# Decode gathers of eight keys a row instead of four, all rotary keys gathered too, and new waits ahead of the gathers

## The reference, cut to what matters

```python
ckv = jnp.concatenate([cache_ckv[layer, pt].reshape(past, KV_LORA), cn], axis=0)   # 4104 x 256
kr = jnp.concatenate([cache_kr[layer, pt].reshape(past, ROPE_DIM), kn], axis=0)    # 4104 x 32
scores = (jnp.einsum("bqhc,btc->bhqt", q_lat, ckv)
          + jnp.einsum("bqhr,btr->bhqt", q_rope, kr)) * MLA_SCALE
p = jax.nn.softmax(jnp.where(mask, scores, NEG_INF), axis=-1)
return jnp.einsum("bhqt,btc->bqhc", p, ckv)
```

## Time and profile before

| | us |
|---|---|
| median of 3 runs | 1426.12 |
| lowest, highest | 1425.38, 1431.34 |
| span of the profiled execution (first to last instruction) | 1420.3 |
| decode stage in it (first score matmul to the last of the values) | 423 to 634.7 |
| mean granted TensorE clock | 0.991 |

### The profile page before, as it was taken

How to read it: one execution, slowest core, us unless ns; L and a number is a source line. 1 busy time by engine, 2 the same in 40 slices (tenths; PEclk the granted TensorE clock), 3 DMA queues, 4 the chain that set the end, 5 groups by cost and what they waited for, 6 DMA issues and landing times.

```text
span 1420.3 us, 27840 instructions
## 1 busy us (share of the span) xinstructions
PE 1366.0 (96%) x11072; PEld 1198.0 (84%) x11072; DVE 851.7 (60%) x1672; ACT 519.4 (37%) x1105; POOL 247.6 (17%) x193
## 2 busy tenths in 40 slices
PE   7999989999988999998999999999999999999997
PEld 7999977766756565566999999999999999999885
DVE  3385358887676556546575857744444455568655
ACT  4221457666361322236333234434333342123100
POOL 3110037775542444401000000000000000000000
PEclk9999999999999999999999999999999999999999
DMA  6643020001372647668122131133333327452722
GB/s 237 201 151 104 1 89 1 1 1 40 127 262 65 199 150 232 217 253 316 46 55 82 45 91 46 45 99 101 110 98 101 119 91 267 159 200 75 267 89 75
DMA packets 108437, 174.36 MB, mean 123 GB/s; under 512 B 14002, under 2 KB 77298, under 8 KB 107028
## 3 DMA queue, kind: packets, MB, share of 16 engines
q1 hardware_dynamic: 98068, 136.92, 29.5%
q0 software_dynamic: 10240, 35.66, 7.7%
HBM read 138.49 MB, written 34.06 MB: 121 GB/s over the span
## 4 chain that ended last, share of the span: by engine, by line
PE 53%; DVE 0%; issue 0%; ACT 0%; DVEq 0%
PE ps L2501 36%; PE ps L2532 10%; PE ps L2566 6%; PE ps L2552 0%; DVE p_h L2874 0%; DVE p_h L2877 0%; DVE p_stats L2861 0%; DVE p_h L2857 0%; PE ps L2542 0%; DVE p_mv L2868 0%; ACT p_rt L2649 0%; DVE p_rs L2872 0%; DVE p_stats L2866 0%; DVE p_stats L2865 0%; DVE p_ve L2870 0%
## 5 line engine op out<-in xcount | busy, mean ns | idle before, releaser
L2501 PE MATMUL ps<-p_x,p_w 128*128 128x272 f32 x4032 | 506.7, 289 | 1.1 <-PEq L2032 0.7
L2501 PEld LDWEIGHTS ps<-p_x,p_w 128*128 128x128 f32 x4032 | 506.4, 188 | 1.4 <-issue 1.4
L2532 PE MATMUL ps<-p_uh,p_w 128*128 128x352 f32 (+1 forms) x576 | 141.9, 327 | 0.0
L1023 POOL TENSOR_SCALAR p_pr<-p_pr,p_rec 128x896 f32<-128x896 f32 (+3 forms) x64 | 112.6, 1769 | 133.0 <-DVE p_rec L987 132.7
L2751 DVE TENSOR_TENSOR p_w<-p_sum,p_w 128x512 fp32r<-128x512 f32 x94 | 65.0, 691 | 117.7 <-ACT p_w L1959 117.6
L1959 ACT ACTIVATE p_w<-p_wr 128x512 fp32r<-128x512 f32 x96 | 60.1, 627 | 131.4 <-PE ps L2532 76.0
L1572 PE MATMUL ps<-p_kT,p_q_rows 32*64 32x256 f32 x2048 | 90.7, 416 | 13.8 <-issue 9.2
L2532 PEld LDWEIGHTS ps<-p_uh,p_w 128*128 128x128 f32 x576 | 101.8, 188 | 0.0
L2532 PE MATMUL ps<-p_ul,p_w 128*128 128x352 f32 (+1 forms) x288 | 94.3, 328 | 0.0
L1572 PEld LDWEIGHTS ps<-p_kT,p_q_rows 32*64 32x64 f32 x2048 | 60.0, 144 | 40.7 <-issue 34.0
L2751 DVE TENSOR_TENSOR p_w<-p_wr,p_w 128x512 fp32r<-128x512 f32 x95 | 65.6, 690 | 38.0 <-ACT p_w L1959 37.4
(11 more groups left out here) (340 smaller groups left out, 2459.8 us busy)
## 6 DMA issues: line engine op xcount, KB each, us to landing
p_wr<-w_in SPq DMA_DIRECT2D x48, 512.0 KB, 3.6
g_kept<-p_slots SPq DMA_DIRECT2D x48, 272.0 KB, 2.5
p_ring<-g_kept SPq DMA_DIRECT2D x16, 544.0 KB, 5.1
p_x<-x_kept SPq DMA_DIRECT2D x6, 1088.0 KB, 8.1
t_kept<-p_t_raw SPq DMA_DIRECT2D x16, 272.0 KB, 2.4
p_x<-t_kept SPq DMA_DIRECT2D x4, 1088.0 KB, 9.3
p_gy<-g_kept SPq DMA_DIRECT2D x8, 544.0 KB, 6.2
p_xs<-x_prompt SPq DMA_DIRECT2D x8, 512.0 KB, 4.2
```

Of the source, the lines that this page charges most:

```text
L1023: nc.gpsimd.tensor_scalar(pr[:, n % PR, 0:w], pr[:, n % PR, 0:w], rec[:, n % PR:n % PR + 1], None, ALU.mult).then_inc(normed, 1)
L2501: last = pe.matmul(ps[:, lo + z, 0:PW], w[:, q % NW, part, t, :], v[:, t, z * PW:(z + 1) * PW], start=(i in STARTS and t == 0 and n == 0), ...
L2532: last = pe.matmul(ps[:, BANK_OF[g % 8], 0:tn], w[:, q % NW, part, t, :], v[:, t0:t0 + tn], start=(t == 0 and z == 0), stop=(t == KH - 1 a ...
```

## The change

A gather now brings rows of eight keys (`ROWK` = 8): 128 rows of 8 KB, 1 MB, for two groups; `h` counts such gathers, `NH` = 32. `NAT` is 10 slots of 1 MB, where it was 19 of 512 KB. The rotary keys come by one gather of 128 rows of 1 KB for each `h`, all on GpSimd; `load_rotary` is gone. In step n GpSimd waits for the whole scoring, gathers `h` = n/2 + 5 (latent and rotary), waits until half of the step's values are done, and gathers `h` = n/2 + 6. `mostly_scored` is gone. VectorE turns `keys(n + 6)` ahead of `keep_scores` in every step from n = 8 on. SyncE loads the page table in eight scattered loads straight into `rows`, and one VectorE instruction finishes it. The late loads of activations come in another order, by the slots' new places.

```diff
-S, LAG, AHEAD, NAT, NSC, RAWR, IN_FLIGHT = 4, G, 6, G + 11, G + 4, 8, 4
+S, LAG, AHEAD, NSC, IN_FLIGHT = 4, G, 6, G + 4, 4
+ROWK, NH, NAT, RAWR = 8, NG // 2, 10, 4
+RPP = PAGE // ROWK
...
+def raw_slot(h):
+
+    return (h + NAT - 2) % NAT
...
 def turn_key_group(dve, e, n):
-    s = n % NAT
-    dve.wait_ge(e["raw_in"][s], 16 * (n // NAT + 1))
+    h, part = n // 2, slice(n % 2 * 4, n % 2 * 4 + 4)
+    dve.wait_ge(e["raw_in"][raw_slot(h)], 16 * (h // NAT + 1))
...
-    rows_in = a["cache_ckv"].rearrange("o n (p a) c -> (o n p) (a c)", a=4)
+    rows_in = a["cache_ckv"].rearrange("o n (p a) c -> (o n p) (a c)", a=ROWK)
...
-            sp.dma_start(e["pages"][:, :], a["page_table"].rearrange("(o b) n -> o (b n)", o=1)
-                         .broadcast_to((P, DECB * NPAGES))).then_inc(pages_in, 16)
+            for j in range(ROWK):
+                src = a["page_table"].rearrange("b (q j) -> j (b q)", j=ROWK)[j:j + 1, :].broadcast_to([RPP, NH])
+                sp.dma_start(e["rows"][RPP * j:RPP * (j + 1), :], src, allow_slow_non_contiguous=True).then_inc(pages_in, 16)
...
-            dve.wait_ge(pages_in, 32)
-            for j in range(4):
-                part = slice(32 * j, 32 * (j + 1))
-                last = dve.tensor_scalar(e["rows"][part, :], e["pages"][part, :].rearrange("p (n z) -> p n z", z=4)[:, :, j],
-                                         32.0, e["row_in"][part, :], ALU.mult, ALU.add)
-            last.then_inc(rows_done, 1)
+            dve.wait_ge(pages_in, 16 * (ROWK + 1))
+            dve.tensor_scalar(e["rows"][:, :], e["rows"][:, :], float(RPP), e["row_in"][:, :], ALU.mult, ALU.add
+                              ).then_inc(rows_done, 1)
...
-X_EARLY = [(B11, 0), (B11, 1), (T1, 1), (T2, 1), (B21, 0)]
+X_EARLY = [(T2, 1), (B21, 0), (B11, 0), (B11, 1), (T1, 1)]
...
-                    if d == NB - 4:
-                        last.then_inc(mostly_scored, 1)
...
-                early_keys = keys_at(n)[:1] if n % G == S and n > S else []
+                early_keys = keys_at(n)[:1] if n > S else []
...
-            for n in range(-S, NG, S):
-                for x in range(n + G, n + G + S):
-                    if NAT <= x < NG:
-                        pool.wait_ge(mostly_scored if n % G else scored, n // S + 1)
-                        pool.wait_ge(pv_done, x - NAT + 1)
-                        gather_pages(nc, a, e, x)
-                for x in range(n + AHEAD + S, n + AHEAD + 2 * S, 2):
-                    if RAWR <= x < NG:
-                        pool.wait_ge(keys_done, (x - RAWR) // 2 + 1)
-                        gather_rotary(nc, a, e, x)
+            def fetch(h):
+                if NAT <= h < NH:
+                    pool.wait_ge(pv_done, 2 * (h - NAT) + 2)
+                    gather_pages(nc, a, e, h)
+                if RAWR <= h < NH:
+                    pool.wait_ge(keys_done, h - RAWR + 1)
+                    gather_rotary(nc, a, e, h)
+
+            fetch(RAWR)
+            for n in range(0, NG, S):
+                pool.wait_ge(scored, n // S + 1)
+                fetch(n // 2 + 5)
+                fetch(n // 2 + 6)
```

More of the change, by code:

```diff
@@ L1061, in key_slot @@
     return (n + S) % (2 * S)
+def raw_slot(h):
+    return (h + NAT - 2) % NAT
 def turn_key_group(dve, e, n):
-    s = n % NAT
-    dve.wait_ge(e["raw_in"][s], 16 * (n // NAT + 1))
+    h, part = n // 2, slice(n % 2 * 4, n % 2 * 4 + 4)
+    dve.wait_ge(e["raw_in"][raw_slot(h)], 16 * (h // NAT + 1))
     return dve.transpose(e["kT"][:, key_slot(n)].rearrange("p a d w -> p (a d w)"),
-                         e["raw_c"][:, s].rearrange("p a c -> p (a c)"))
+                         e["raw_c"][:, raw_slot(h), part].rearrange("p a c -> p (a c)"))
 def turn_rotary(dve, e, n):
[L1074 to L1078, removed]
+    h = n // 2
+    dve.wait_ge(e["raw_r_in"][h % RAWR], 16 * (h // RAWR + 1))
+    x = key_slot(n)
+    return dve.transpose(e["rT"][:, x:x + 2].rearrange("p x a w -> p (x a w)"), e["raw_r"][:, h % RAWR, :])
 def load_queries(sp, k, e, b):
@@ L1098, in load_rotary @@
-def load_rotary(sp, a, e, regs, n):
-    s = n % RAWR
-    sp.load(regs, e["pages"][0:1, 4 * n:4 * n + 4])
-    for j in range(4):
[L1103 to L1114, removed]
+        nc.gpsimd.wait_ge(e["raw_in"][raw_slot(x)], 16 * (x // NAT + 1))
@@ L1459, in x_free @@
         lo = x_at + X_AT[blk, part] * X_BLOCK
-        assert e["raw_r_end"] <= lo and lo + X_BLOCK <= e["end"] + 16 * NAT * KVL
+        size = 4 * ROWK * KVL
+        assert e["raw_r_end"] <= lo and lo + X_BLOCK <= e["end"] + NAT * size
         lo -= e["end"]
-        slots = range(max(lo, 0) // (16 * KVL), (lo + X_BLOCK - 1) // (16 * KVL) + 1)
-        return max(max(n for n in range(NG) if n % NAT == s) for s in slots) + 1
+        slots = range(max(lo, 0) // size, (lo + X_BLOCK - 1) // size + 1)
+        return 2 * max(max(h for h in range(NH) if raw_slot(h) == s) for s in slots) + 2
     late["x_free"] = x_free
@@ L1517, in _ @@
         def _(sp):
-            regs = [sp.alloc_register(f"page{j}") for j in range(4)]
-            for n in range(RAWR + 1, NG, 2):
-                sp.wait_ge(keys_done, (n - RAWR) // 2 + 1)
-                load_rotary(sp, a, e, regs, n)
-                b = n // G
-                if n % G == 3 and b >= 2:
-                    sp.wait_ge(scored, (b - 1) * G // S)
-                    load_queries(sp, k, e, b)
-                b, late_by = divmod(n - (NG - G - 3), 6)
-                if 0 <= b < KV_EARLY and not late_by:
-                    load_mem(sp, a, late["kv"][:, b], b, k["kv_early"][b])
+            for b in range(2, DECB):
+                sp.wait_ge(scored, (b - 1) * G // S)
+                load_queries(sp, k, e, b)
+                if b >= DECB - KV_EARLY:
+                    x = b - (DECB - KV_EARLY)
+                    sp.wait_ge(keys_done, NH - 9 + 3 * x)
+                    load_mem(sp, a, late["kv"][:, x], x, k["kv_early"][x])
             mid = list(range(KV_EARLY, KV_EARLY + KV_MID))
             for blk, part in X_EARLY:
-                if mid and late["x_free"](blk, part) > NG - LAG:
+                if mid and late["x_free"](blk, part) >= NG - LAG:
                     sp.wait_ge(scored, NG // S)
@@ L1614, in values @@
                         last = pe.matmul(ps[e * R:(e + 1) * R, to, 0:KVL], held[:, n % 2, f, e * R:(e + 1) * R],
-                                         raw_c[:, n % NAT, 2 * e + f, :], start=(g == 0 and f == 0 and e == 1),
+                                         raw_c[:, raw_slot(n // 2), 4 * (n % 2) + 2 * e + f, :], start=(g == 0 and f == 0 and e == 1),
                                          stop=(g == G - 1 and f == 1))
```

43 lines of the change are left out of this document (21 added, 22 removed).

## The result

| | before | changed |
|---|---|---|
| median (4 runs each, same chip) | 1427.22 us | 1389.30 us |
| lowest, highest | 1425.38, 1431.34 | 1385.89, 1391.74 |
| ratio of the times, 95% interval | | 0.974 (0.9722 to 0.9757) |
| span of the profiled execution | 1420.3 | 1389.9 (its own time: 1391.74) |

37.9 us less, 2.6%. The forecast was 1396 (1387 to 1418), faster.

The account below looks back on a forecast made before the run. TensorE, busy 96% of the span, was taken as the bound, starved by gathers in decode; -26.9 (pairs) - 3.3 (opening) = -30.2 us from the 1420.3 span gives 1390.1, plus 5.8 is 1395.9, say 1396 (1387 to 1418).

Parts of the forecast that it names:

- What is lost and an undisturbed pair (20.1 us): Decode stage: a pair of steps costs 20.1 us undisturbed; six pairs took 160.6 against 120.8, so 39.8 us are lost.
- Gather instructions starve TensorE, the bytes don't: Decode scoring: while GpSimd issues gathers back to back, hardly any new instruction reaches TensorE; DMA traffic is not the cause.
- 8 KB rows cost GpSimd 1.02 us: Latent gathers: 128 rows of 8 KB take GpSimd what 128 rows of 4 KB do, 1.02 us.
- 2.35 us lost in a pair: Decode pairs: stalls of 0.6 us after first steps and 1.75 after second, in place of 6.6 a pair; saves 26.9 us.
- No clock falls in the pairs: Decode pairs: the remaining stalls are too short for TensorE's clock to fall; clock 1.00 from 450 on.
- Opening, 3.3 us: First scoring: one rotary gather under it instead of four saves 5.0 us; stalls of about 1.0 and 0.7 us leave 3.3.
- Early keys, row indices, SyncE: 0: Keys turned ahead of scores in first steps, scattered row-index loads, and SyncE's dropped rotary loads and reordered activations: each costs 0.
- From span to median: Whole kernel: the median of 1426.12 lies 5.8 us above the profiled span, and this difference stays.
- The stock of 49 matmuls and 6 per further gather: TensorE during a run of gathers: it lives on some 49 queued matmuls and about 6 more per further gather.
- Gathers of 2 us: Rival, 10%: gathers of 8 KB rows take GpSimd 2 us; 1427 us, give or take 7.
- The traffic rival: Rival, 6%: DMA traffic starves TensorE, so moving transfers behind the scoring puts them under the next one; slower, 1441 us.
- the gathers starve more: Rival, 20%: ScalarE's copies late or the clock lowered once a pair; saves 12 to 22 us, say 1411 us.

Follow-up runs that it names:

- run with another order: Changed kernel with a step's four gathers ordered latent, rotary, rotary, latent, so only the last waits for the step's values; 1388.70 us, 0.9731 of the kernel before.
- run with both edits: Changed kernel with gathers ordered latent, rotary, rotary, latent and waiting for a mark 48 matmuls ahead of the scoring's end; 1392.16 us, 0.9774 of the kernel before.
- nearly the same kernel: Changed kernel with first steps' keys turned after the scores are kept, as in the kernel before; 1377.04 us, 0.9931 of the kernel before.

## Why the prediction was right, and where

- **What is lost and an undisturbed pair (20.1 us).** Right: 20.4 us with plain loads, 20.2 on the chip without starvation.
- **Gather instructions starve TensorE, the bytes don't.** Shown on one chip by the two runs that took one and left the other. But it does not hold everywhere: in the first comparison and in the first two sets the kernel before takes 1427, 1422 and 1428 us and the traces there show the stalls; in the third it takes 1385, and with four gathers a step they are absent under the same gathers, with six they are later and shorter. On that chip the 26.9 us forecast for the pairs could not have been saved; that the comparison ran on another is luck. On the chip of the first set the stalls need gather instructions, and in the third set these are not enough. What else is needed stays open.
- **8 KB rows cost GpSimd 1.02 us.** Right, 1.01 to 1.03.
- **2.35 us lost in a pair.** 22.35 us is the mean of the four pairs with all gathers: 2.2 lost. The 1.75 us after second steps came as 1.8 (3.64 against 1.86); the 0.6 after first steps came as 0.45. Over all six pairs 132.2 - 120.8 = 11.4 us are lost, against 12.9. Saved 28.5 us against 26.9.
- **No clock falls in the pairs.** Right: 1.00 throughout.
- **Opening, 3.3 us.** 4.5: a term sized a third too small. From its start to the start of the second scoring the opening took 6.13 us, where it had taken 11.16: the 5.0 saved are right. What was wrong is the 1.7 us of stalls set against them: the next two stretches grew by 0.3 and 0.2 us only (7.14 to 7.46, 12.35 to 12.54).
- **Early keys, row indices, SyncE: 0.** Row indices right. VectorE still waits for gathers, 11.8 us in 10 places against 11.6 in 11 before (423 to 620 and 635), but no wait of TensorE for keys or kept scores appears from 440 to 600. No run takes back the SyncE part alone.
- **Sum.** 1390.1 as a span, 1389.9 measured: closer than it deserves. The decode stage gave 2.8 us more than the sum and began 1.2 us sooner (421.81 against 422.99), and what follows it took 3.8 us longer (809.8 from 580.10 to the end, against 806.0 from 614.26). Half a clock for 10.24 us in there is chance, and the next profile, which lacks it, is 3.9 us shorter. That these three cancel is luck.
- **From span to median.** The 5.8 us that I added are the mis-sized term: a profiled execution's time is 1.84 us above its span (1391.74 against 1389.9), so the one profiled before, whose time is not on record, took about 1422.1, some 4 us below its median and below the fastest of the four runs (1425.38). With 1.84 the forecast would have been 1391.9 against 1389.3. This also explains most of the 37.9 us: 34.3 are the difference of the spans without the half clock (1420.3 and 1386.0).
- **The stock of 49 matmuls and 6 per further gather** sized the stalls after second steps well (1.75 against 1.8 us). The run with another order suggests that the 6 belong to the pauses, which is argued and not shown, and the run with both edits shows that the model is too narrow: VectorE and ScalarE are held up too.
- **Rivals.** Gathers of 2 us and late row indices did not come. The traffic rival fell to the run with short rows. That the gathers starve more did not come with four a step; with six it did (clock 0.89).

## What to carry to other kernels

Count GpSimd's gather instructions, not their bytes: 1.02 us for 128 rows of 256 bytes or of 8 KB, and in the traces of two of the three sets the other engines get few instructions while a run of them lasts. Put them where those engines have slow work and their next instructions already under way, and check each engine, since a run that is moved off one lands on another. Before a few per cent are put down to a kernel, run both versions on more than one chip: the gain is 2.6 and 2.7% in two comparisons and was 0.7% for nearly the same kernel on the third set's chip.

## What the runs showed of the hardware

- That the starvation differs from chip to chip, or from time to time: 1379.5 to 1389.5 us for the kernel before in 23 runs on one chip, 1420 to 1431 in 20 runs of the first comparison and the other sets, with gathers of the same 1.02 us. The Trainium skill ("Runtime: NRT & Kernel Launch", Instruction fetch mechanics) describes instruction fetch as hidden; in the third set the trace with four gathers a step agrees (20.20 us of 20.20 busy), the one with six does not (1.56 us idle inside the rotary matmuls), and in the other sets it does not either.
- That VectorE and ScalarE can be held up until a run of gathers is over: they start 0.80 and 0.86 us after its last one, as TensorE does (0.77 to 0.85).
- That a trace records transfers of 16 KB on an instruction queue, and that in the third set's run with six gathers TensorE goes on 1.4 to 1.5 us after one of them has ended, four times out of four.
- That SyncE's loads with addresses from registers take 0.86 us each in a long row, against 0.43 for the plain query loads (1.71 us for four).
